# A norm's gain vector multiplied into the weight tiles on GpSimd, and normed tokens split straight from PSUM

## The reference

```
x  = x + w0 * result[dest0] + w1 * result[dest1]        (end of the first block)
h  = x * rsqrt(mean(x * x) + eps) * norm_mix_pre        (RMS norm with a gain per channel)
z  = h @ w_in                                           (1024 x 3084, input of four mixers)
```

## Time and profile before

| | before |
|---|---|
| median of 3 runs | 3046.01 us (3043.59 to 3047.04) |
| the profiled execution's own time | 3051.29 us |
| its span, first to last instruction | 3049.5 us |
| mean granted clock of TensorE | 0.942 of full |
| TensorE matmul busy | 2712.1 us (89%) |
| VectorE busy | 2087.3 us (68%) |
| ScalarE busy | 1379.9 us (45%) |
| GpSimd busy | 591.1 us (19%) |

### The profile page before, as it was taken

The page is one execution under the profiler, slowest core; times in us unless marked ns, Lnnn a source line. Parts: engine busy times, 40 slices in busy tenths (PEclk is TensorE's granted clock), DMA queues, the critical chain, the costliest instruction groups (busy, mean ns, idle before and its releaser), DMA issues. The chain is left out here.

```text
span 3049.5 us, 41793 instructions
## 1 busy us (share of the span) xinstructions
PE 2712.1 (89%) x14250; PEld 2261.5 (74%) x14250; DVE 2087.3 (68%) x2635; ACT 1379.9 (45%) x2179; POOL 591.1 (19%) x386
## 2 busy tenths in 40 slices
PE   5999996789959999999499997867888799999997
PEld 5888785677858888888477786755776688887886
DVE  3997516865469999999535254766664888887677
ACT  4122325642238888887423213466434433333444
POOL 1232221711001111111222110101100533432000
PEclk9999998999969999999799997978999899999999
DMA  3112227733269999999512221031114122232734
GB/s 99 38 49 76 79 73 264 271 125 135 74 227 413 416 415 414 413 417 376 199 49 69 73 73 44 2 125 30 29 63 152 28 83 84 83 83 63 252 104 159
DMA packets 269183, 474.18 MB, mean 155 GB/s; under 512 B 35230, under 2 KB 154053, under 8 KB 269029
## 3 DMA queue, kind: packets, MB, share of 16 engines
q1 hardware_dynamic: 239700, 402.33, 37.3%
q10 hardware_dynamic: 20480, 39.85, 3.5%
q0 software_dynamic: 8848, 29.96, 2.9%
HBM read 379.72 MB, written 92.35 MB: 155 GB/s over the span
## 5 line engine op out<-in xcount | busy, mean ns | idle before, releaser
L2145 DVE TENSOR_TENSOR e_w_lo<-e_ring,e_w_hi 128x1024 fp32r<-128x1024 f32 x384 | 446.7, 1218 | 47.3 <-ACT e_w_hi L2072 47.3
L2072 ACT CAST e_w_hi<-e_ring 128x1024 fp32r<-128x1024 f32 x384 | 377.1, 1048 | 35.4 <-PE banks L2005 28.5
L2003 PE MATMUL banks<-e_w_hi,e_xT_hi 128*128 128x512 f32 x512 | 203.4, 397 | 0.0
L2005 PE MATMUL banks<-e_w_hi,e_xT_lo 128*128 128x512 f32 x512 | 200.6, 392 | 0.0
L2004 PE MATMUL banks<-e_w_lo,e_xT_hi 128*128 128x512 f32 x512 | 200.3, 391 | 0.0
L956 DVE SCALAR_TENSOR_TENSOR conv<-x_first,vectors,conv 128x1024 f32<-128x1024 f32 x120 | 187.3, 1561 | 9.7 <-issue 0.9
L940 POOL TENSOR_TENSOR p_w_lo<-p_w,p_w_hi 128x1024 fp32r<-128x1024 f32 (+1 forms) x48 | 107.7, 2245 | 340.9 <-ACT p_w_hi L866 340.9
L2881 PE MATMUL banks<-u_sums,u_w_hi 128*128 128x512 f32 (+1 forms) x364 | 140.6, 386 | 10.2 <-DVE u_sums L3060 9.0
L1946 POOL COPY e_pick<-expert_index 128x1 int32 x31 | 64.6, 2085 | 417.7 <-PE banks L1996 407.1
L804 PE MATMUL banks<-h_hi,p_w_hi 128*128 128x512 f32 x352 | 140.5, 399 | 1.3 <-POOL p_w_lo L940 1.3
L2883 PE MATMUL banks<-u_sums,u_w_lo 128*128 128x512 f32 (+1 forms) x364 | 140.3, 385 | 0.0
(11 more groups left out here) (659 smaller groups left out, 7457.1 us busy)
## 6 DMA issues: line engine op xcount, KB each, us to landing
e_ring<-in_w_gate_e_dram SPq DMA_DIRECT2D x128, 512.0 KB, 6.1
e_ring<-in_w_up_e_dram SPq DMA_DIRECT2D x128, 512.0 KB, 6.3
e_ring<-in_w_down_e_dram SPq DMA_DIRECT2D x128, 512.0 KB, 5.3
u_w<-in_ffn_w_up_dram SPq DMA_DIRECT2D x44, 512.0 KB, 5.8
expert_results<-nothing SPq DMA_DIRECT2D x1, 16384.0 KB
expert_results<-e_y ACTq DMA_DIRECT2D x32, 512.0 KB, 7.7
p_w<-in_w_in_dram SPq DMA_DIRECT2D x24, 512.0 KB, 3.8
t_raw<-in_ffn_w_down_dram SPq DMA_DIRECT2D x11, 1024.0 KB, 7.7
```

The lines of the kernel that those rows point to most:

```text
L2003: mm(bank, xT_hi[:, b, k, :], w_hi[:, part, cols], start=(k == 0), stop=False)
L2005: last = mm(bank, xT_lo[:, b, k, :], w_hi[:, part, cols], start=False, stop=(k == KT - 1))
L2072: nc.scalar.copy(w_hi[:, part, :], experts.ring[:, slot, :]).then_inc(w_rounded, 1)
L2145: tt(w_lo[:, part, :], experts.ring[:, slot, :], w_hi[:, part, :].bitcast(F32), ALU.subtract).then_inc(w_split, 1)
```

## The change

The gain is taken out of the tokens' path and multiplied into the weights, since h @ w = (x * rstd) @ (gain * w). `CombinedNorm` gets its own `turn`, `round_off` and `rest`: ScalarE rounds the transposed tokens from their banks, VectorE subtracts from the banks, `times_gain` and the buffer `whole` are gone, and the banks come free when a token tile is parted. The order changes with it: `mean(0)` and `rate(0)` come before `add(2)`, and ScalarE takes the root of pair q+1 before it rounds token tile 2q. In `project_columns` each weight tile is multiplied in place by the gain before ScalarE rounds it: VectorE does so for tiles 0 and 1, GpSimd for all others. GpSimd's order is: gathers, multiply tiles 2 and 3, then for each tile n its split and behind it the multiply of tile n+2, which waits for that tile's load. ScalarE's `fill` waits for the multiply (`w_gained`) in place of the load.

```diff
--- before.py
+++ after.py
@@ -449,14 +449,36 @@
     AHEAD = False
 
 
-    def __init__(self, K, tag, x, rstd, gain, hi, lo, whole, xn, y, junk, weights, dest, results, keep):
-        super().__init__(K, tag, x, rstd, gain, hi, lo, whole, xn)
+    def __init__(self, K, tag, x, rstd, gain, hi, lo, xn, y, junk, weights, dest, results, keep):
+        self.K, self.x, self.rstd, self.gain, self.hi, self.lo, self.xn = K, x, rstd, gain, hi, lo, xn
+        self.scaled, self.turned, self.rounded, self.parted = (K.sem(f"{tag}_{n}") for n in ("scaled", "turned", "rounded", "parted"))
         self.y, self.junk, self.weights, self.dest, self.results, self.keep = y, junk, weights, dest, results, keep
         self.SLOTS = y.shape[1]
         self.gathered = [K.sem(f"{tag}_gathered{t}") for t in range(NT)]
         self.added, self.squared, self.meaned, self.rooted, self.rated = (K.sem(f"{tag}_{n}") for n in
             ("added", "squared", "meaned", "rooted", "rated"))
         self.x_kept = K.sem(f"{tag}_x_kept")
+
+    def bank(self, t):
+        return self.K.ps[:, 4 + 2 * (t % 2):6 + 2 * (t % 2), :].rearrange("p c (k n) -> p (c k) n", n=P)
+
+    def turn(self, pe, t):
+        pe.wait_ge(self.scaled, t + 1)
+        if t >= 2:
+            pe.wait_ge(self.parted, t - 1)
+        for k in range(KT):
+            mm = self.K.nc.tensor.transpose(self.bank(t)[:, k, :], self.xn[:, t % 2, k * P:(k + 1) * P], self.K.const("ident"))
+        mm.then_inc(self.turned, 1)
+
+    def round_off(self, act, t):
+        act.wait_ge(self.turned, t + 1)
+        self.K.nc.scalar.activation(self.hi[:, :, t * P:(t + 1) * P], self.bank(t), ACT.Copy).then_inc(self.rounded, 1)
+
+    def rest(self, dve, t):
+        tokens = slice(t * P, (t + 1) * P)
+        dve.wait_ge(self.rounded, t + 1)
+        self.K.nc.vector.tensor_tensor(self.lo[:, :, tokens], self.bank(t), self.hi[:, :, tokens].bitcast(F32),
+                                       ALU.subtract).then_inc(self.parted, 1)
 
     def on_gpsimd(self, pool):
         for t in range(NT):
@@ -495,9 +517,9 @@
         self.scale(act, 1)
         self.square(act, 1)
         for q in range(PAIRS):
-            self.round_off(act, 2 * q)
             if q + 1 < PAIRS:
                 self.root(act, q + 1)
+            self.round_off(act, 2 * q)
             self.round_off(act, 2 * q + 1)
             if q + 1 < PAIRS:
                 act.wait_ge(self.rated, q + 2)
@@ -531,14 +553,12 @@
         PAIRS = NT // 2
         self.add(dve, 0)
         self.add(dve, 1)
-        self.add(dve, 2)
         self.mean(dve, 0)
         self.rate(dve, 0)
+        self.add(dve, 2)
         self.add(dve, 3)
         for q in range(PAIRS):
             t = 2 * q
-            self.times_gain(dve, t)
-            self.times_gain(dve, t + 1)
             if q + 1 < PAIRS:
                 self.mean(dve, q + 1)
             self.rest(dve, t)
@@ -562,8 +582,8 @@
     w_in = weight.rearrange("o (k p) n -> p (o k) n", p=P)
     widths = [max(at + n for _, n, at in pieces) for pieces, _ in slabs]
     landed = [K.sem(f"{tag}_landed{b}") for b in range(2)]
-    rounded, split, projected, chunked, kept, gates_kept = (K.sem(f"{tag}_{n}") for n in
-        ("rounded", "split", "projected", "chunked", "kept", "gates_kept"))
+    w_gained, rounded, split, projected, chunked, kept, gates_kept = (K.sem(f"{tag}_{n}") for n in
+        ("w_gained", "rounded", "split", "projected", "chunked", "kept", "gates_kept"))
     SLOTS = 4
     stored = [K.sem(f"{tag}_stored{b}") for b in range(SLOTS)] if stores else []
     with ExitStack() as scope, nc.Block() as block:
@@ -572,6 +592,12 @@
         stage = K.sb(scope, f"{tag}_stage", [P, SLOTS, HALF]) if stores else None
         sizes = [KT * P] * U + [m for m in widths for _ in range(KT)]
         pieces_of = [pieces for pieces, *_ in units] + [pieces for pieces, _ in slabs for _ in range(KT)]
+
+        def with_gain(n):
+            if n < U:
+                return w[:, n % 2].rearrange("p (k n) -> p k n", k=KT), norm.gain.unsqueeze(2).to_broadcast([P, KT, P])
+            k = (n - U) % KT
+            return w[:, n % 2, 0:sizes[n]], norm.gain[:, k:k + 1].to_broadcast([P, sizes[n]])
 
         @block.sync
         def _(sp):
@@ -630,15 +656,12 @@
         @block.scalar
         def _(act):
             act.sem_inc(kept, 4)
-            loads = [0, 0]
             done, sent, in_slot = [4], [0], [0] * SLOTS
 
             def fill(n):
                 if n >= U + C:
                     return
-                if n >= 2:
-                    loads[n % 2] += 16 * len(pieces_of[n])
-                    act.wait_ge(landed[n % 2], loads[n % 2])
+                act.wait_ge(w_gained, n + 1)
                 nc.scalar.activation(w_hi[:, n % 2, 0:sizes[n]], w[:, n % 2, 0:sizes[n]], ACT.Copy).then_inc(rounded, 1)
 
             def keep(dst, bank, func, scale, targets):
@@ -703,15 +726,30 @@
         @block.gpsimd
         def _(pool):
             norm.on_gpsimd(pool)
+            loads = [0, 0]
+
+            def times_gain(n):
+                loads[n % 2] += 16 * len(pieces_of[n])
+                pool.wait_ge(landed[n % 2], loads[n % 2])
+                tile, gain = with_gain(n)
+                nc.gpsimd.tensor_tensor(tile, tile, gain, ALU.mult).then_inc(w_gained, 1)
+
+            times_gain(2)
+            times_gain(3)
             for n, m in enumerate(sizes):
                 if n < 2:
                     continue
                 pool.wait_ge(rounded, n + 1)
                 nc.gpsimd.tensor_tensor(w_lo[:, n % 2, 0:m], w[:, n % 2, 0:m], w_hi[:, n % 2, 0:m].bitcast(F32), ALU.subtract) \
                     .then_inc(split, 1)
+                if n + 2 < U + C:
+                    times_gain(n + 2)
 
         @block.vector
         def _(dve):
+            for n in range(2):
+                tile, gain = with_gain(n)
+                nc.vector.tensor_tensor(tile, tile, gain, ALU.mult).then_inc(w_gained, 1)
             for n in range(2):
                 dve.wait_ge(rounded, n + 1)
                 nc.vector.tensor_tensor(w_lo[:, n], w[:, n], w_hi[:, n].bitcast(F32), ALU.subtract).then_inc(split, 1)
@@ -4271,7 +4309,7 @@
             with ExitStack() as shadow:
                 beside = RwkvGates(K, shadow, z, zm, W, scratch, Z["mlstm"][:, :, 0:3])
                 gathered = z[:].rearrange("p j n -> p (j n)")[:, 0:8 * D].rearrange("p (t c n) -> p t c n", c=2, n=D)
-                norm = CombinedNorm(K, "n3", x, K.row_squares, K.vec("norm_mix_pre_2", 0, KT), h_hi, h_lo, W["kk"][:], gates[:, 0:2, :],
+                norm = CombinedNorm(K, "n3", x, K.row_squares, K.vec("norm_mix_pre_2", 0, KT), h_hi, h_lo, gates[:, 0:2, :],
                                     gathered, gates[:, 2, :], *combining)
                 project_columns(K, "z", K.A["w_in_2"], h_hi, h_lo, units, slabs, norm, z_first, gates=Z["gates"], stores=stores, beside=beside)
             h_scope.close()
```

## The result

The changed kernel takes 3056.36 us, median of 9 runs (3050.31 to 3060.09), against 3047.04 of the kernel before, 9 runs (3043.59 to 3052.47): ratio 1.0026, 95% interval 1.0015 to 1.0036. By the medians it is slower by 9.3 us. The ratio is not the quotient of the medians (that would be 1.0031); it stands for 7.9 us, its interval for 4.6 to 11.0. So slower is clear, and the sum's 12.7 lies above the interval. The profiled execution took 3059.79, its span is 3057.7 (3049.5 before), and the mean granted clock is 0.942 in both.

A forecast was written before the change was run, and what follows sets the result against it. VectorE was taken to be busiest in the norm, TensorE to pace units and slabs, in a serial stage. Norm -1.0, last slab +12.4 and clock +1.3 gave +12.7: median 3046.0 to 3059, range 3051 to 3068.

The forecast's parts named there:

- The last slab, +12.4: 256-wide slab: each tile costs a closed round of split, load and multiply, 5.4 against TensorE's 2.88; +12.4, bounds +8.1 to +16.4.
- TensorE's clock, +1.3: Last slab, chunk 7: a 2.6 us stretch at the lower clock after an idle gap costs half; +1.3, bounds 0 and +2.9.
- Units and first slab, 0: The 18 units and 512-wide slab: GpSimd's multiply fits under TensorE's pace; 0, with a bound of +3 for the units.
- The norm, -1.0: Norm in all: +0.3-0.4-1.2+0.3=-1.0 us, bounds -2.9 and +0.9.
- Pairs: Norm: a token pair takes 10.5 where it took 10.7; two pairs save 0.4.
- Last pair: Norm's last pair: TensorE's wait of 1.24 for the splits goes; -1.2.
- Start: Norm's start: +0.3 from mean(0) ahead of add(2), +0.3 from VectorE's weight multiplies stretching GpSimd's gather issues.
- lower bound: Norm, -2.9: third pair's first unit at the full clock, 1.6 less, and 0.3 without stretched gathers.
- upper bound: Norm, +0.9: the last pair gains 0.3 only, and gathers cost twice.
- A: Last slab: loads stay hidden, so the 12.4 and the 1.3 fall away; 3045, chance 0.04.
- B: Norm: VectorE's work, not the round trip, sets the pace; four pairs lose 2.35 each, -9.4; 3050, chance 0.09.
- C: Slabs: GpSimd's multiply is dearer, at twice the split's price, or meets VectorE more often; +24, 3070, chance 0.13.

The follow-up runs named there:

- the order alone: Changed kernel, but GpSimd multiplies tile n directly ahead of its split (from tile 4 on): 3047.49 us, ratio 0.999 to the kernel before.
- the loop alone: Norm of the kernel before, gain included, plus the changed kernel's weight multiplies in its order, by ones: 3061.6 us, ratio 1.0035 to before.
- one load: Changed kernel, but each chunk of the last slab comes in one transfer in place of four: 3055.46 us, ratio 1.0021 to the kernel before.
- the norm's chain: Changed kernel, GpSimd multiplying n directly before its split, VectorE one add of pair q+2 before mean(q+1), ScalarE's root behind the first rounding: 3042.4 us, ratio 0.9976.
- the norm once more: Changed kernel, GpSimd multiplying n directly before its split, ScalarE's root behind first rounding, add before mean only in the second pair's turn: 3043.78 us, ratio 0.9988.

## Why the prediction was right

The forecast was its likeliest case, and the time came out slower by 9.3 by the medians (7.9 by the ratio) where the sum said 12.7. The mechanism is the one forecast; the sum was too high by the round of the last slab and by the clock. By its steps:

**The last slab, +12.4: +10.3.** Mechanism and place are shown: the loss goes with the order alone, comes with the loop alone, halves with one load. The size was off in the round, 4.95 for 5.4. The multiply was taken at the split's price with a share of collisions, 0.95, and took 0.67; the split 0.86 for 0.95; the wait with the issues 3.46, where 3.4 and 0.1 of hops were taken. Five rounds of 0.45 less are 2.3, and 12.4-2.3=10.1 is what was measured within 0.2.

**TensorE's clock, +1.3: about 0.** The clock did fall, to 0.50 from 1841.5 to 1844.7, after the fifth gap, the longest (2.33). But it fell on the sixth chunk, whose matmuls ended when the split of the seventh did, at 1844.68: the slow stretch filled what would have been the next gap. TensorE's next matmul starts at 1844.74 without a wait, and from 1844.9 the clock is 1.00 again:

```profile
1844.74 0.39 PE L648 MATMUL banks<-z_w_hi,h_hi 128*128 128x256 f32 x1
```

The Trainium skill's rule on oscillation (TensorE: Matmul & The Clock Gate, HAM oscillation), by which each tile could start low, is for longer waits than the 1.00 to 2.33 here and did not come out: the clock fell after one gap of five, and 1.3 us into that chunk, not at its start.

**Units and first slab, 0: 0.** TensorE's pace stays, with no new wait. The -0.77 in the table is less than what the granted clock ahead of the slabs makes of it from profile to profile: where that clock was 1.00 throughout (the norm's chain, the norm once more, one load) the row "units and first slab" takes 269.2, in all others, with stretches of 0.89 to 0.94, 272.2 to 274.0. The multiplies of tiles 2 and 3 lay in GpSimd's idle time (1524.19, two of 1.9), as said.

**The norm, -1.0: -1.2.** That the sum is near is luck: its terms were off by +0.5, -0.4 and -0.3. Pairs: 10.31 each for 10.5 (10.7 before), -0.8 where -0.4 stood. Last pair: from the third pair's begin to the rounding of tile 2 12.68 for 14.15, -1.5 where -1.2 stood. Start: +1.1 where +0.3 and +0.3 stood. Without VectorE's multiplies the first pair began 0.7 sooner than before (1.0 in the kernel with no multiply), so the new order saves at the start, which I had costed at +0.3, and the multiplies cost 1.8 there, which I had costed at 0.3. The 1.8 is rough: four kernels with the same start of the norm began that pair at 32.27 to 33.57, the two without the multiplies at 31.06 and 31.32. The 1.6 that the lower bound had for a third pair at the full clock is borne out: 12.68 fell to 11.2 in those two. The upper bound was added up wrongly, though: its terms give +0.2, not +0.9, which moves the forecast's upper end by 0.7 and nothing else.

**The rivals.** A (loads hidden) fell: all multiplies in the last slab wait for a DMA, though under the other order A's outcome is what happens (last slab 27.96). B (VectorE paces the norm) fell: 2.4 of 9.9 us went from VectorE's pair and the pair shrank by 0.4. So the rule that the busiest engine is relieved first (the Trainium skill, Perfetto Trace Analysis, Identifying the Most-Contended Engine) misleads here: waits for ScalarE took the place, 1.24 for the square and 1.18 for the rounding. C (dearer multiply) fell: 612 to 795 ns a chunk against 722 to 1396 for the split.

Still open: what sets that clock ahead of the slabs, which goes with some 3 to 5 us of a profiled stage.

## What to carry to other kernels

On an engine that works its queue off in order, an operation that waits for a newly issued load must not stand ahead of work on a tile that has landed already, when the end of that work lets the next load be issued. Queue the wait behind that work, and the same multiplies are nearly free (last slab 27.96 to 29.75 in the five kernels with that order, for 38.29). Look at the narrowest stage for it, where a tile's compute (2.88) is shorter than the closed round (4.95); wide stages hide the same fault, as the first slab did with 5.43 a chunk. Work taken off an engine that is 96% busy buys little (0.4 of 2.4 us a pair here) until the wait in its own chain is filled with other work, as the reordered adds did (norm 61 for 66).

## What the runs showed of the hardware that was not expected

- GpSimd's multiply of a tile by an operand of stride zero is cheaper than its subtract of two full tiles: 0.61, 1.04 and 1.90 us for 256, 512 and 1024 wide, against 0.72, 1.29 and 2.40 (at 256 the shortest of the changed kernel, else its medians). The Trainium skill (GPSIMD Engine Reference, Elementwise) gives some 2.6 cycles an element for two inputs, at 1.2 GHz an estimate of 2.2 us for 1024: the split lies near it, the multiply below. The rows of the first slab and of the units:

```profile
L735 POOL TENSOR_TENSOR z_w<-z_w,vectors x7: 612/1040/1040, 1773.8 to 1810.7; 128x512 f32<-128x512 f32 x5, 128x256 f32<-128x256 f32 x2
L735 POOL TENSOR_TENSOR z_w<-z_w,vectors x19: 1040/1897/3505, 1545.3 to 1757.0; 128x1024 f32<-128x1024 f32 x16, 128x512 f32<-128x512 f32 x3
```

- A gather's issue on GpSimd takes 0.94 us and up to 1.96 while VectorE runs an operation with two tiles as inputs. The Trainium skill (GPSIMD Engine Reference, Specifications) says that GpSimd shares its SBUF interfaces with VectorE, with contention where a VectorE instruction has two inputs in SBUF; the trace agrees. It is not the number of operations that counts: two splits back to back stretched one issue by 0.33, two splits 3.5 us apart stretched two by 0.4 and 1.0. What sets the amount was not found.
